# Moving recurrence scans, a buffer and one head's scores in a two-block hybrid kernel

## The reference, cut to what matters

```
# retention, per head: q, k rotated by cos/sin; scores = (q . k) * decay; inner = scores . v
q = _rope(q, ROPE_BASE_A); k = _rope(k, ROPE_BASE_A) * DK_A ** -0.5
scores = einsum('bhcd,bhed->bhce', qi, ki) * dmat
inner  = einsum('bhce,bhev->bhcv', scores, vi)

# recurrence of the hybrid layer, over the 256 tokens, 1024 features
r = sigmoid(xc @ wa + ba); i = sigmoid(xc @ wx + bx)
a = exp(-8 * r * softplus(-lam));  u = sqrt(1 - a*a) * (i * xc)
h[t] = a[t] * h[t-1] + u[t];       y_rnn = h * gelu(rnn_gate)

# attention of the hybrid layer: keys outside an indexer's 64 best get -inf, then softmax
gates = sigmoid(g + gate_b)
merged = gates[0] * (y_rnn @ w_o_rnn) + gates[1] * (y_attn @ w_o_attn)
```

## Time and profile before

| | us |
|---|---|
| median of 3 runs | 948.28 (946.54 to 949.96) |
| profiled execution | 948.28, its span 946.6 |
| PE busy | 920.7 (97%) |
| PE weight loads busy | 842.2 (89%) |
| DVE busy | 581.1 (61%) |
| ACT busy | 495.9 (52%) |
| POOL busy | 91.9 (10%) |
| mean granted clock of PE | 0.991 of full speed |

### The profile page before, as it was taken

One profiled execution on the slowest core, in us unless ns is written; L12 is line 12 of the kernel. 1 busy time (PEld: TensorE's weight loads), 2 busy tenths in 40 slices (PEclk: granted clock), 3 DMA queues, 4 the chain that ended last, 5 costly groups with the idle time before them and its releaser, 6 DMA issues.

```text
span 946.6 us, 14021 instructions
## 1 busy us (share of the span) xinstructions
PE 920.7 (97%) x5964; PEld 842.2 (89%) x5964; DVE 581.1 (61%) x762; ACT 495.9 (52%) x610; POOL 91.9 (10%) x68
## 2 busy tenths in 40 slices
PE   5999999998999999999989999999899999999998
PEld 5898887888999999998877899999899899998886
DVE  4776566558876666666476758776656665554441
ACT  5444444435666666664436466777653455554330
POOL 0110100002001111111020000111200012220000
PEclk8999999999999999999999999999999999999999
DMA  9634444642553443345544525332243545556520
GB/s 371 253 134 178 177 153 167 195 142 90 200 185 113 151 150 145 140 179 194 182 183 156 200 90 183 129 124 100 96 170 137 210 146 179 180 186 213 181 108 23
DMA packets 24526, 153.63 MB, mean 162 GB/s; under 512 B 3088, under 2 KB 3472, under 8 KB 8464
## 3 DMA queue, kind: packets, MB, share of 16 engines
q1 hardware_dynamic: 22144, 146.81, 43.5%
q10 hardware_dynamic: 2160, 5.40, 1.8%
q0 software_dynamic: 160, 0.52, 0.1%
HBM read 151.67 MB, written 1.05 MB: 161 GB/s over the span
## 4 chain that ended last, share of the span: by engine, by line
PE 89%; ACT 4%; DVE 4%; issue 2%; DMA 0%; ACTq 0%; DVEq 0%
PE ps L302 26%; PE ps L304 26%; PE ps L303 26%; ACT w_hi_ring L803 1%; PE ps L352 1%; PE ps L515 1%; PE ps L516 1%; PE ps L536 1%; PE ps L690 1%; DVE w_lo_ring L1208 1%; ACT c_p L1167 1%; PE ps L526 1%; PE ps L424 1%; PE ps L642 1%; PE ps L679 1%
## 5 line engine op out<-in xcount | busy, mean ns | idle before, releaser
L1208 DVE TENSOR_TENSOR w_lo_ring<-w_raw,w_hi_ring 128x2048 fp32r<-128x2048 f32 x148 | 346.6, 2351 | 234.0 <-ACT w_hi_ring L803 226.6
L803 ACT ACTIVATE w_hi_ring<-w_raw 128x2048 fp32r<-128x2048 f32 x148 | 281.8, 1911 | 132.7 <-PE ps L304 131.1
L302 PE MATMUL ps<-xT_hi,w_hi_ring 128*128 128x256 f32 x776 | 223.2, 288 | 4.8 <-DVE w_lo_ring L1208 4.8
L303 PE MATMUL ps<-xT_lo,w_hi_ring 128*128 128x256 f32 x776 | 220.4, 284 | 0.0
L304 PE MATMUL ps<-xT_hi,w_lo_ring 128*128 128x256 f32 x776 | 220.4, 284 | 0.0
L302 PEld LDWEIGHTS ps<-xT_hi,w_hi_ring 128*128 128x128 f32 x776 | 149.7, 193 | 5.8 <-DVE w_lo_ring L1208 5.1
L303 PEld LDWEIGHTS ps<-xT_lo,w_hi_ring 128*128 128x128 f32 x776 | 149.8, 193 | 0.7
L304 PEld LDWEIGHTS ps<-xT_hi,w_lo_ring 128*128 128x128 f32 x776 | 149.7, 193 | 0.0
L302 PE MATMUL ps<-w_hi_ring,xT_hi 128*128 128x512 f32 (+1 forms) x272 | 107.1, 394 | 0.0
L304 PE MATMUL ps<-w_hi_ring,xT_lo 128*128 128x512 f32 (+1 forms) x272 | 104.5, 384 | 0.0
L303 PE MATMUL ps<-w_lo_ring,xT_hi 128*128 128x512 f32 (+1 forms) x272 | 104.5, 384 | 0.0
(11 more groups left out here) (308 smaller groups left out, 1575.7 us busy)
## 6 DMA issues: line engine op xcount, KB each, us to landing
w_raw<-in_a_w_in SPq DMA_DIRECT2D x24, 1024.0 KB, 5.0
w_raw<-in_w_ff_in SPq DMA_DIRECT2D x16, 1024.0 KB, 4.9
w_raw<-in_w_ff_out SPq DMA_DIRECT2D x16, 1024.0 KB, 4.9
w_raw<-in_b_w_uq SPq DMA_DIRECT2D x16, 576.0 KB, 4.0
w_raw<-in_a_w_out SPq DMA_DIRECT2D x8, 1024.0 KB, 4.8
w_raw<-in_b_w_gate SPq DMA_DIRECT2D x8, 1024.0 KB, 4.8
w_raw<-in_kv_w_up SPq DMA_DIRECT2D x8, 1024.0 KB, 4.8
w_raw<-in_b_w_out SPq DMA_DIRECT2D x8, 1024.0 KB, 5.1
```

What stands on the lines that cost most here:

```text
L302: k.T.matmul(out, lh, rh, start=start, stop=False, skip_group_check=True)
L303: k.T.matmul(out, lh, rl, start=False, stop=False, skip_group_check=True)
L803: k.A.activation(k.hi[:, u % RING, :], k.raw[u % RING][:, :], ACT.Copy).then_inc(k.s["w_hi"], 1)
L1208: k.V.tensor_tensor(k.lo[:, u % RING, :], k.raw[u % RING][:, :], k.hi[:, u % RING, :].bitcast(F32), ALU.subtract).then_inc(k.s["w_lo"], 1)
```

## The change

Three edits. (1) In `pe_retention` the scores stand between the two value units for head 0 too, as for the others; the function `pe_retention_scores` is written into its place. (2) c_aa gets the 2048 words in which c_rl and c_p lie, and c_rgw no longer holds it; ACT's wait for the scans ahead of the tanh of n = 8 goes. (3) DVE's eight scans move from behind the bias of group 0 (n = 6) to four at n = 5 and four at n = 6, ahead of that bias, which now waits for them, since it writes c_p.

```diff
-    k.c_p = k.place("c_p", [P, 4, 3 * P])
-    k.place("c_rl_rest", [P, 512])
+    k.c_aa = k.place("c_aa", [P, KD, S])
...
-    k.c_rl = k.place("c_rl", [P, RL, 3 * P], at=k.at["c_p"])
+    k.c_rl = k.place("c_rl", [P, RL, 3 * P], at=k.at["c_aa"])
...
-    k.c_aa = k.place("c_aa", [P, KD, S], at=k.at["c_rgw"])
+    k.c_p = k.place("c_p", [P, 4, 3 * P], at=k.at["c_aa"])
...
     token_major(k, u + 2, k.xT, 0, 4, 512, v_out, True, False)
-    if h:
-        pe_retention_scores(k, h)
+    T.wait_ge(s["a_rope"], h + 1)
+    for e, cols in enumerate((slice(0, 2 * P), slice(2 * P, 3 * P))):
+        for n in range(2):
+            m = T.matmul(ps[:, 0, cols], k.a_qk[:, 2 + n, e * P:(e + 1) * P], k.a_qk[:, n, e * P:2 * P],
+                         start=e == 0 and n == 0, stop=n == 1, skip_group_check=True)
+    m.then_inc(s["a_scored"], 1)
     token_major(k, u + 3, k.xT, 4, 4, 512, v_out, False, True)
-    if h == 0:
-        pe_retention_scores(k, h)
...
-            if n == 8:
-                A.wait_ge(s["rec_scan"], KD)
...
+        elif n in (5, 6):
+            if n == 5:
+                V.wait_ge(s["rec_u"], 1)
+            for c in range(4 * (n - 5), 4 * (n - 5) + 4):
+                V.tensor_tensor_scan(k.c_rr[:, c, :], k.c_aa[:, c, :], k.c_ig[:, c, :], 0.0, ALU.mult, ALU.add).then_inc(s["rec_scan"], 1)
...
             dve_attention_scores(k, (n - 6) // 2)
-        if n == 6:
-            V.wait_ge(s["rec_u"], 1)
-            for c in range(KD):
-                V.tensor_tensor_scan(k.c_rr[:, c, :], k.c_aa[:, c, :], k.c_ig[:, c, :], 0.0, ALU.mult, ALU.add).then_inc(s["rec_scan"], 1)
...
         V.wait_ge(s["selected"], 1)
+        V.wait_ge(s["rec_scan"], KD)
```

More of the change, by code:

```diff
@@ L416, in pe_retention @@
     token_major(k, u + 5, k.xT, 4, 4, 512, g_out, False, True)
[L419 to L426, removed]
 def pe_turn_head(k, h, banks):
```

## The result

The changed kernel takes 954.37 us (median of 12 runs, 951.15 to 957.57) against 947.63 us (12 runs, 946.54 to 950.66): ratio 1.0066, interval 1.0052 to 1.0082, so +6.3 us. It is slower, as forecast; the forecast was +4.3. (A difference in us is here the ratio's, times the median of the kernel before.) The profiled execution has a span of 954.0 us, 7.4 more than before.

The account below looks back on a forecast made before the run. TensorE was taken as nearly always busy, so its stalls are paid in full, with the hybrid stage's chain of waits running through DVE and ACT. Retention 1.9 plus hybrid 2.4 gave +4.3 on 948.28: 952.6 us, range 950.0 to 955.5.

Parts of the forecast that it names:

- Part 1, "+1.9": Retention, head 0: scores ahead of value unit 3 make PE wait 1.9 us for the rotated q and k.
- rival (a): PE's clock also falls at the new retention stall, costing 1.7 us more: 954.3 us; chance 0.13.
- The floor of 0.8 us: Retention, head 0: PE's stall is at least 0.8 us, since cosine work can't start before q and k are copied.
- Part 2, "+2.4": Hybrid stage: scans ahead of the score bias make the chain 3.1 us late, less 0.65 us of room: +2.4 us.
- bias of group 0 late by 5.0: Hybrid stage: the bias, queued behind eight scans and lo(9), comes at 640.3 against 635.29, 5.0 us later.
- the small step 0.7 longer: Hybrid stage: the 8-column last step of the maxima loses 0.7 us beside POOL's c_gel product.
- PE's first wait 5.7: Hybrid stage: PE stands 5.7 us before the first group's transposes, waiting for the exponentials.
- lo(10) at 2.29: Hybrid stage: DVE's lo half of unit 10 no longer meets POOL and loses its 2.95 us, taking 2.29, not 5.24.
- the second transposes without a wait: Hybrid stage: PE arrives at 669.4, just behind c_ya, so the old 4.2 us wait is gone.
- the third waiting 2.4 - 1.5 = 0.9: Hybrid stage: late c_ya of group 1 leaves +2.4 us, against a balance of +1.5 at the second transposes.
- 1.7 us behind the long wait: Hybrid stage: PE's clock falls to half behind the wait before the first transposes, losing 1.7 us.
- Rival (c): Hybrid stage: faster, as lo(10) avoids POOL and PE's wait and clock loss shrink: 945.9 us; chance 0.07.

Follow-up runs that it names:

- part 1 alone: Kernel before with only head 0's scores moved between the two value units, scans and buffers as before: 952.29 us, ratio 1.0045.
- With PE kept busy: As part 1 alone, plus eight unread 128x512 products on PE ahead of the wait for the rotated tensor: 952.36 us, ratio 1.0031 to the kernel before.
- with the table out of the way: DVE waits for the decay table only ahead of its use: with part 1 alone 949.79 us; on the whole change, c_gel also waiting for group 0's maxima, 951.48 us.
- The later c_gel: Kernel before with one wait more, POOL's product c_gel waiting for the maxima of group 1: 945.09 us, ratio 0.9956.
- part 2: Kernel before with only the buffer changes and the scans ahead of group 0's bias, head 0's scores as before: 950.00 us, ratio 1.0014.
- the order alone: Kernel before with only the scans moved to n=5 and n=6, buffers and ACT's wait for the scans kept: 950.97 us, ratio 1.0019.

## Why the prediction was right, and where it was short

**Part 1, "+1.9".** The wait was sized right: 2.0 us in the profile, 2.4 in part 1 alone. The step that failed is the sum's omission of the clock: it put it at nothing, and 1.7 us were measured. "A stall of 1.9 us lies between none and the 3.1 us that did it; rows decide nothing between" was true, and I then gave the fall 0.13 as rival (a). It happened in both profiled executions with this wait, and part 1 alone costs +4.3 us by its ratio. Wait plus clock, 1.9 + 1.7 + 2.4 = 6.0, is within the measured interval (+4.9 to +7.8 us); the forecast's +4.3 is below it. So the kernel did what rival (a) says (954.3), and the time of 954.37 us is inside the stated range because the range was drawn to take that rival in. The starting point helped a little: the forecast counts from 948.28, and from the 947.63 of the 12 runs its 952.6 would be 951.9. With PE kept busy the stretch gave the 1.6 us back. How often the clock falls behind this wait can't be read from two profiles; the changed kernel's runs spread over 6.4 us, those before over 4.1.

**The bounds of part 1.** The floor of 0.8 us for the stall was named from the copy of q and k, and held within 0.1: with the table out of the way PE was 0.55 + 0.16 = 0.7 us late, in part 1 and in the whole change alike (the stretches grew by 0.85 and 0.82). What sets it is POOL's sine product, which ended at 31.12, 2.2 us after the cosine's. The expectation for that experiment, a wait of 1.3 us, was further off than my own floor.

**Part 2, "+2.4".** +2.50 in the full change, +2.38 alone. Its inner steps, forecast and measured: bias of group 0 late by 5.0, 645.27 - 635.29 - 4.89 (the shift at c_ig) = 5.1; the small step 0.7 longer, 0.63; PE's first wait 5.7, 5.6; lo(10) at 2.29; the second transposes without a wait; the third waiting 2.4 - 1.5 = 0.9, 0.8. The Trainium skill's exclusive lock (SBUF — State Buffer, section "SBUF: two separate sides") is borne out down to an operation of 8 columns: 0.80 us beside POOL's product, 0.17 when that was moved.

**The clock in part 2.** I took 1.7 us behind the long wait; the profile shows half clock from 651.0 to 657.9, of which 3.6 us lie behind the wait's end at 654.3, so 1.8 us. As forecast, it stands in for the loss that the old wait brought.

**What gives back.** Rival (c) named the right mechanism, lo(10) free of POOL, for a kernel that paid 5 us for it. The later c_gel takes it for nothing, and with 4.2 us is the one gain of this study.

**Whole times (partly open).** Those of part 2 and of its order (+1.3, +1.8) lie under the +2.4 of the stretch. The executions on record account for it. Those whose mean granted clock was highest form a group of their own: 0.996 and 946.9 us in 1 of 23 executions of the kernel before (946.8 to 947.1 in 5 of 29 of the next experiments), 0.995 and 948.9 to 949.4 us in 6 of 12 of part 2 and 5 of 12 of the order. Within these groups the difference is 2.0 to 2.6 us. The other executions took 948.2 to 950.7 us before, 950.6 to 952.8 with part 2 and 950.7 to 952.8 with the order, again 2.1 to 2.5 more. The medians differ by less because more of part 2's executions are in the first group. Why they are is open: the profiles show that the clock behind waits elsewhere costs more or less from one execution to the next (below), and no run separates what sets it.

## What to carry to other kernels

Before you move a piece of work that costs nothing where it stands, find what runs beside it (here ACT's exponentials beside the scans) and ask if it still does so afterwards. Price a new wait of the matrix engine with the clock behind it, even when it is shorter than those seen to trigger the fall. And look at when POOL runs a long two-input operation: moving it from beside a DVE split to behind the maxima of group 1 was worth 4.2 us here, more than part 2 cost.

## What the runs showed of the hardware

- The clock fell behind waits of 2.0 and 2.4 us; waits of 0.5, 0.6 and 1.5 us left it up. The fall began 1.3 us after the matmuls had come back in the full change (36.6 against 35.4) and 0.3 us after in part 1 alone (35.5 against 35.2), and lasted 3.4 us in both.
- The same wait does not cost the same each time. The 3.1 us wait at about 220 us had 3.4 us of half clock in 8 of the 12 profiles (at most 1.7 us lost) and none in that of part 1 alone. In three it had 6.8: in that of the order alone from 218.6 to 225.5, of which 5.7 lie behind the wait's end at 219.7, so 2.9 lost. The 4.1 us wait at about 500 us had 3.4 us of half clock in 5 profiles and 6.8 in 7.
- A DVE step of 8 columns with two SBUF inputs, 0.17 us alone, stood 0.63 us behind POOL's product, 0.87 in the profile of the order alone (1.04 us long); DVE operations that read PSUM and one SBUF tensor (the bias, 1.28 us for two) ran at their usual length beside it.
